# A bounded forget gate as a clamped logit with two softplus terms, and feed-forward products over high and low rows at once as 512 columns

## The reference

```python
log_f = jnp.logaddexp(jnp.log(lb), jnp.log1p(-lb) + jax.nn.log_sigmoid(f_logit))
k = -jnp.expm1(log_f)                       # hgrn2_mixer, then cumsum(log_f) and the chunks
...
def swiglu(h, w13, w2):                     # h 256 x 1024, w13 1024 x 5632, w2 2816 x 1024
    gate, up = jnp.split(h @ w13, 2, axis=-1)
    return (jax.nn.silu(gate) * up) @ w2
```

## Time and profile before

| | |
|---|---|
| median of 3 runs | 2272.09 us |
| the profiled execution's own time | 2272.5 us |
| its span | 2270.7 us |
| PE busy | 2141.9 us, 94% |
| DVE busy | 1372.8 us, 60% |
| ACT busy | 996.0 us, 44% |
| mean granted clock of PE | 0.981 of 2.4 GHz |

### The profile page before, as it was taken

One profiled execution on the slowest core, in us unless ns is written; L12 is line 12 of the kernel. 1 busy time (PEld: TensorE's weight loads), 2 busy tenths in 40 slices (PEclk: granted clock), 3 DMA queues, 4 the chain that ended last, 5 costly groups with the idle time before them and its releaser, 6 DMA issues.

```text
span 2270.7 us, 29738 instructions
## 1 busy us (share of the span) xinstructions
PE 2141.9 (94%) x12707; PEld 1879.8 (83%) x12707; DVE 1372.8 (60%) x1667; ACT 996.0 (44%) x1324; POOL 99.7 (4%) x121
## 2 busy tenths in 40 slices
PE   6999999899798999899999999999998998999998
PEld 5988878888787998687778799989986877877997
DVE  4657865757876555555675555565555666745554
ACT  4544535344444434444444444443434443544432
POOL 0100100100010000000000000000000000000000
PEclk9999999999999999999999999999999999999999
DMA  7453234353235555435545355555544444543552
GB/s 247 131 188 118 87 130 168 111 189 116 70 130 184 180 188 174 136 113 164 193 147 180 114 201 186 196 176 187 185 154 139 135 163 168 185 149 134 191 186 93
DMA packets 192412, 356.84 MB, mean 157 GB/s; under 512 B 8284, under 2 KB 85144, under 8 KB 192280
## 3 DMA queue, kind: packets, MB, share of 16 engines
q1 hardware_dynamic: 189400, 344.46, 45.3%
q0 software_dynamic: 2880, 10.49, 1.4%
HBM read 353.87 MB, written 1.05 MB: 156 GB/s over the span
## 4 chain that ended last, share of the span: by engine, by line
PE 80%; DVE 10%; ACT 4%; issue 3%; DMA 1%; POOL 1%; SPq 0%; POOLq 0%; ACTq 0%; DVEq 0%
PE bank L1864 14%; PE bank L1860 14%; PE bank L1870 14%; PE bank L1887 8%; PE bank L1884 8%; PE bank L1890 8%; DVE raw_r L2334 3%; PE bank L1908 3%; PE bank L2028 2%; PE bank L1925 2%; ACT high L2137 2%; PE bank L1899 1%; PE bank L1946 1%; POOL stat L2824 1%; DVE units L2430 1%
## 5 line engine op out<-in xcount | busy, mean ns | idle before, releaser
L2334 DVE TENSOR_TENSOR raw_r<-raw,high 128x2048 fp32r<-128x2048 f32 (+1 forms) x308 | 694.8, 2273 | 99.6 <-ACT high L2137 99.6
L2137 ACT ACTIVATE high<-raw 128x2048 fp32r<-128x2048 f32 (+1 forms) x308 | 581.2, 1896 | 258.8 <-PE bank L1870 218.5
L1860 PE MATMUL bank<-high,units_r 128*128 128x512 f32 x1648 | 663.9, 403 | 21.3 <-DVE units L2790 11.7
L1864 PE MATMUL bank<-high,units_r 128*128 128x512 f32 x1648 | 651.6, 395 | 24.2 <-DVE units_r L2355 12.4
L1870 PE MATMUL bank<-raw_r,units_r 128*128 128x512 f32 x1648 | 443.9, 391 | 0.2
L1884 PE MATMUL bank<-units_r,high 128*128 128x256 f32 x1600 | 399.1, 285 | 0.0
L1887 PE MATMUL bank<-units_r,high 128*128 128x256 f32 x1600 | 395.8, 283 | 0.0
L1864 PEld LDWEIGHTS bank<-high,units_r 128*128 128x128 f32 x1648 | 314.2, 191 | 92.6 <-DVE units_r L2358 16.0
L1860 PEld LDWEIGHTS bank<-high,units_r 128*128 128x128 f32 x1648 | 313.5, 190 | 88.9 <-issue 21.3
L1870 PEld LDWEIGHTS bank<-raw_r,units_r 128*128 128x128 f32 x1648 | 312.2, 190 | 67.3 <-DVE raw_r L2334 1.6
L1884 PEld LDWEIGHTS bank<-units_r,high 128*128 128x128 f32 x1600 | 308.0, 193 | 1.3
(11 more groups left out here) (247 smaller groups left out, 1849.1 us busy)
## 6 DMA issues: line engine op xcount, KB each, us to landing
raw<-in_ffn_w_dram SPq DMA_DIRECT2D x132, 1024.0 KB, 5.1
raw<-in_w_in_dram SPq DMA_DIRECT2D x108, 1024.0 KB, 5.1
raw<-in_w_out_dram SPq DMA_DIRECT2D x24, 1024.0 KB, 5.0
raw<-in_cross_wkv_dram SPq DMA_DIRECT2D x16, 1024.0 KB, 5.0
raw<-in_w_branch_dram SPq DMA_DIRECT2D x12, 1024.0 KB, 4.9
raw<-in_cross_wq_dram SPq DMA_DIRECT2D x8, 1024.0 KB, 5.2
...
```

The lines of the kernel that those rows point to most:

```text
L1860: pe.matmul(o, h.high(k0 + k)[:, span], p.hi[k][:, cols], start=start and k == 0, stop=False, skip_group_check=True)
L1864: pe.matmul(o, h.low(k0 + k)[:, span], p.hi[k][:, cols], start=False, stop=False, skip_group_check=True)
L2137: done = act.activation(high, raw, ACT.Copy)
L2334: done = dve.tensor_tensor(low, raw, high.bitcast(F32), ALU.subtract)
```

## The change

In the feed-forward parts, `up(j)` uses a new step `wide` instead of `ch`. The high weights stream 512 columns in one matmul, the high rows and the low rows together (`whole` makes one operand from the two units; `pairs` now sorts them by number so that the distance is positive), and the two results stand side by side in a bank. The 8 matmuls with low weights stay at 256 columns. So a tile has 16 matmuls instead of 24 and fills a bank alone. A new step `fold` adds the halves: ACT copies the right half out, DVE adds the left half to it. Tanh, SiLU and `glu` then read a unit instead of a bank. `up` takes four banks at a time instead of two.

In the gate of layer 1, log f is written as clamp(f, ln lb, 0) - ln(1+exp(-|f|)) + ln(1+exp(-|f - ln lb|)): ACT makes, beside ln(1+exp(-|f|)), also ln(1+exp(-|f - ln lb|)) for each bank, with a third table of bounds `NEG_LNLB`; DVE clamps the logit with two `tensor_scalar` of 256 for each bank, and `bounded` is three DVE operations on 128 x 1024 in one step. `gate_f` has two rests instead of five. One more unit (`t2`) is taken.

```diff
+    def whole(self, k, units_r):
+        a, b = (u.i for u in self.pairs[k // 4])
+        return units_r[:, a:b + 1:b - a, k % 4 * 256:k % 4 * 256 + 256]
...
-        return Rows([(self.U.take(), self.U.take()) for _ in range(n)])
+        return Rows([sorted((self.U.take(), self.U.take()), key=lambda u: u.i) for _ in range(n)])
...
+    def mm_wide(self, name, p, h, banks):
+        for c in range(p.n // P):
+            self.work += p.k * (512 + 256)
+            self.do("wide", name=name, p=p, c=c, bank=banks[c], h=h, ends=c == p.n // P - 1)
+            if c == p.n // P - 1:
+                self.done(p)
+            yield 0
+
+    def fold(self, name, need, banks, dst, after):
+        for c, b in enumerate(banks):
+            self.do("fold", name=name, c=c, need=(need, c), bank=b, dst=dst[:, c * 256:c * 256 + 256], after=after)
+            self.B.give(b, ("folded", name, c))
+        return ("folded", name, len(banks) - 1)
...
             def gate_f():
+                t2 = bounds = None
+                if l == 1:
+                    t2 = U.take()
+                    bounds = [a[:, 4 * hg:4 * hg + 4] for a in (LNLB, LN1M, NEG_LNLB)]
                 for q, (b, pr) in enumerate(fb):
-                    do("forget", name=H, q=q, need=pr, bank=b, k_=k_, tl=tl, tc=tc, lns=q == 0, last_set=q == 1 and l == 0)
+                    do("forget", name=H, q=q, need=pr, bank=b, k_=k_, tl=tl, tc=tc, t2=t2, bounds=bounds)
                     B.give(b, ("logf", H, q))
                     yield "rest"
                 if l == 1:
...
-                    do("bounded", name=H, phase=0, k_=k_, tl=tl, tc=tc, bounds=bounds)
-                    yield "rest"
-                    do("bounded", name=H, phase=1, k_=k_, tl=tl, tc=tc, bounds=bounds)
-                    yield "rest"
-                    do("bounded", name=H, phase=2, k_=k_, tl=tl, tc=tc, bounds=bounds)
+                    do("bounded", name=H, k_=k_, tl=tl, tc=tc, t2=t2, bounds=bounds)
+                    U.give(t2, ("bounded", H))
...
-            bg, bu = B.take(), B.take()
-            yield from plan.mm_ch(f"{N}.g{j}", plan.weight(w13, 0, 8, 256 * j, 256), h, [bg])
-            s = plan.silu(f"{N}.s{j}", [("prod", f"{N}.g{j}", 0)], tmp.ap[:, 0:512], bg.ap, tmp.after)
-            B.give(bg, s)
...
+            bg = [B.take(), B.take()]
+            ((_, p),) = plan.weight(w13, 0, 8, 256 * j, 256)
+            yield from plan.mm_wide(f"{N}.g{j}", p, h, bg)
+            g_ = plan.fold(f"{N}.g{j}", ("prod", f"{N}.g{j}"), bg, tmp.ap[:, 0:512], tmp.after)
+            s = plan.silu(f"{N}.s{j}", [g_], tmp.ap[:, 512:1024], tmp.ap[:, 0:512], tmp.after)
+            bu = [B.take(), B.take()]
...
+    def wide(name, p, c, bank, h, ends, **_):                      # PE
...
+            pe.matmul(bank.ap.rearrange("p (a s) -> p a s", a=2), p.hi[k][:, c * P:c * P + P], h.whole(k, m.units_r),
+                      start=k == 0, stop=False, skip_group_check=True)
+        hold.wait_ge(*at(("wlow", p.i)))
+        for k in range(p.k):
+            product = pe.matmul(bank.ap[:, 0:256], p.lo[k][:, c * P:c * P + P], h.high(k), start=False,
+                                stop=k == p.k - 1, skip_group_check=True)
...
+    def fold(name, c, need, bank, dst, after, **_):                # ACT
...
+        act.activation(dst, bank.ap[:, 256:512], ACT.Copy).then_inc(*mark(s.acopy, ("half_out", name, c)))
...
+            for i in range(2):                                     # ACT, forget
+                c = q * 2 + i
+                beyond = act.activation(t2.ap[:, c * 256:c * 256 + 256], bank.ap[:, i * 256:i * 256 + 256], ACT.Abs,
+                                        bias=bounds[2][:, c:c + 1], scale=1.0)
...
+            act.activation(t2.ap[:, sl], t2.ap[:, sl], ACT.Exp, bias=0.0, scale=-1.0).then_inc(*mark(s.expd))
+            hold.wait_ge(*last(s.expd))
+            act.activation(t2.ap[:, sl], t2.ap[:, sl], ACT.Ln, bias=1.0, scale=1.0).then_inc(
...
+                clamped = dve.tensor_scalar(tc.ap[:, c * 256:c * 256 + 256], bank.ap[:, i * 256:i * 256 + 256],
+                                            bounds[0][:, c:c + 1], 0.0, ALU.max, ALU.min)
...
+    def bounded(name, k_, tl, tc, t2, bounds, **_):                # DVE
+        hold.wait_ge(*at(("logf", name, 1)))
+        dve.tensor_tensor(tc.ap, tc.ap, tl.ap, ALU.subtract).then_inc(*mark(s.vstep))
+        dve.tensor_tensor(h3(k_.ap, 4), h3(k_.ap, 4), bc(bounds[1], 256), ALU.subtract).then_inc(
...
+        dve.tensor_tensor(tc.ap, tc.ap, t2.ap, ALU.add).then_inc(*mark(s.vout, ("bounded", name)))
...
+    def fold(name, c, bank, dst, **_):                             # DVE
+        hold.wait_ge(*at(("half_out", name, c)))
+        dve.tensor_tensor(dst, bank.ap[:, 0:256], dst, ALU.add).then_inc(*mark(s.vout, ("folded", name, c)))
```

102 lines of the change are left out of this document (51 added, 51 removed).

## The result

The changed kernel takes 2255.52 us (median of four runs, 2254.12 to 2256.11) against 2273.06 for the kernel before on the same basis (four runs, 2271.39 to 2276.54). The ratio is 0.992, 95% interval 0.9903 to 0.9937, so it is faster by 0.6 to 1.0%. The forecast was 2251.4, range 2244 to 2264. The profiled execution has a span of 2253.9 us, 16.8 less than before; 21.1 was forecast.

A forecast was written before the change was run, and what follows sets the result against it. PE, busy 94% of the span, was taken as the bound. From 2272.5 us, -15.4 (feed-forward), -2.7 and -0.5 (first heads) and -2.5 (second heads) sum to -21.1, giving 2251.4 us, range 2244 to 2264.

The forecast's parts named there:

- The bound and the main mechanism: Feed-forward parts: only PE's pace counts, and fewer matmuls shorten the time; PE busy 140.00 of 140.00 us.
- the 13.3 ns beside its columns: Feed-forward matmuls on PE: each costs a fixed 13.3 ns whatever its width, beside one column per cycle.
- The first rival: Feed-forward: the fixed 13.3 ns doesn't go, so the gate alone gives 2266.8 us; 7% together with the skill-figure case, 2263.9.
- The term of -15.4 us: Feed-forward parts: 144 `wide` tiles at 2.773 us instead of 2.880, 0.107 us less each, 15.4 us in all.
- one piece later: Feed-forward: a gate product's bank is wanted again 5.55 us after its last product, so no wait was taken.
- the sign named in the prediction: Feed-forward parts: the forecast counts as wrong if they give less than 13 us, or the time exceeds 2264.
- The term of the first heads, -2.7 and -0.5: Layer 1's gate, first four heads: PE starts at 410.2 instead of 412.87, -2.7 us; the clock after the wait, -0.5.
- The second heads, -2.5: Layer 1's gate, second four heads: earlier waits grow, later ones go, net -2.5 us, bounds +5 and -6.
- The second rival: Layer 1's gate goes the wrong way: scan ahead of scores costs 5 us, first heads give nothing; 2262.1 us, 12%.
- the sum of both terms, -5.7: Layer 1's gate: -2.7 and -0.5 for the first four heads with -2.5 for the second four.
- ACT and DVE at nothing, no bank dry: Feed-forward: the new copies and additions hide behind PE, cost nothing; banks running dry, 2312 us, was given 5%.

The follow-up runs named there:

- halves: The changed kernel with each matmul of 512 columns made as two of 256 with the same weight; 2267.16 us, ratio to the kernel before 0.9971.
- gate_only: The changed kernel with the feed-forward code of before put back, so only the gate is changed; 2266.62 us, ratio to the kernel before 0.9975.
- rests: The changed kernel with three resting places put ahead of the bounded gate of layer 1; 2255.72 us, ratio to the kernel before 0.9922.
- contig: The changed kernel with the 512 columns read contiguously from one unit, so wrong rows are multiplied; one run of 2254.72 us.
- wide_only: The changed kernel with the old gate put back, so only the feed-forward parts are changed; 2261.71 us, ratio to the kernel before 0.9951.
- no_fold: The changed kernel without the fold's copies on ACT and additions on DVE, PE's work the same; one run of 2257.23 us.
- the three loaded kernels: The changed kernel with the fold's copy moved or repeated, as dve_fold, dve_stress and act_stress; one run each, 2257.65, 2282.27 and 2260.90 us.
- act_stress: The changed kernel with the fold's copy on ACT made four times; one run of 2260.90 us.
- grouped: The changed kernel with both tiles' matmuls of 512 columns run before both tiles' of 256 for each weight piece; 2255.78 us, ratio to the kernel before 0.9921.
- dve_fold: The changed kernel with the fold's copy made by DVE instead of ACT; one run of 2257.65 us.
- dve_stress: The changed kernel with the fold's copy made by DVE instead of ACT, three times over; one run of 2282.27 us.

## Why the prediction was right, and what it had wrong

**The bound and the main mechanism: right.** PE's pace alone counts in the feed-forward parts, a removed matmul takes the 13.3 ns beside its columns with it, less the cost of a change of width, and the gain is 0 when the matmuls are put back with all else left as it is (`halves`). The first rival is out. By the fixed remainder that the Trainium skill gives for warm matmuls back to back ("TensorE: Matmul & The Clock Gate", section "Wait — 56ns, not 53.3ns?", about 2.5 ns) the 1152 removed matmuls would be worth an estimated 2.9 us. `halves` against the changed kernel measures 12.8, so the runs don't agree with it for this pattern, in which each matmul loads its weights.

**The term of -15.4 us: too large.** A `wide` tile was costed at 8 x 226.7 + 8 x 120.0 = 2.773 us and takes 2.79. The 226.7 came from a `tok` block that follows another one, a row in which the width doesn't change; a `wide` tile changes it every 16 matmuls. The first `tok` block behind a `ch` tile would have shown it: 2.74 us. All 36 `up` together went from 414.9 to 402.0 us, 12.8 less (the medians of one, 11.515 and 11.148 us, would make it 13.2). Of the other 0.5 us to the 12.3 found, 0.35 are a wait behind the first fold (740.74), and the rest I can't assign. The wait stands where the prediction's "one piece later" doesn't hold: the second `up` of a part takes the banks of the product right before it. So the sign named in the prediction, less than 13 us from these parts, came true, by 0.7 us, from a mis-sized term.

**The term of the first heads, -2.7 and -0.5: a little small in sum, and the two parts are off by more.** PE starts `same` 4.0 us earlier, not 2.7. ACT's table load starts at 400.44 instead of 401.0 to 401.2, and the second high part didn't wait for its piece (3.70 us for both from 404.14), so that the copies begin at 407.74. Behind this wait of 1.76 us the clock stayed up: over 412 to 424 it is 1.00, before 0.79. That gave 1.9 us more by 411.10 (417.04 before), where -0.5 was taken. But a new wait of 1.76 us at 419.85, which was not foreseen, took them back, and from there on the lead is 4.0 us. That the clock could be left at -0.5 without harm is luck.

**The second heads, -2.5: right** (-2.55 measured), with waits grown to 5.25 and 4.06 and those behind them gone, as told. The second rival, the gate going the wrong way, is out with `gate_only` at 0.9975. `rests` supports the reason, eight passes of 1024 become five. But the same gate is worth -3.7 in all in `halves`, -5.7 in `gate_only`, -6.6 in the changed kernel and -7.6 in `contig`, and the old gate of `wide_only` is 1.5 us ahead of its like: the sum of both terms, -5.7, is met no better than that.

**ACT and DVE at nothing, no bank dry: right** but for the 0.35 us above, by `no_fold` and the three loaded kernels. The end of a part cost nothing either: PE's wait there is 1.73 us before and after. `act_stress` shows that it isn't far from costing something.

**Missing: the +2.3 us between the feed-forward parts of layer 0.** The stretch from the wait of 1.73 us behind the first part to the one of 2.89 us ahead of the second (898.48 to 1297.51 before, 889.24 to 1290.59 after) holds the same instructions. It takes 399.0 us before, 399.0 in `gate_only` and 398.8 in `halves`, in which the feed-forward parts are as long as before, and 401.4 after, 401.4 in `wide_only` and `contig`, 401.6 in `grouped`. The same stretch of layer 1 takes 398.1 to 398.5 in all of these but `grouped` (398.9). The granted clock is at half for 20.5 us of the stretch in both traces, but at other places: before for 6.8 us at 932.4 and 1133.7 and for 3.4 at 976.7 and 1154.2, after for 3.4 at 925.6 and 1253.3 and for 6.8 at 966.6 and 1127.0. What counts is what PE has to do there. At 1253.3 it has matmuls back to back. The first row is the changed kernel, the second the same place before (first the length and PE's busy time with its matmuls, at the end the granted clock, DMA share and GB/s):

```profile
1253.30:1256.70 3.40, 3.33 (x15) 3.36 (x16) 0.00 (x0) 0.46 (x1) 0.00 (x0) 0.50 0.45 171
1261.60:1265.00 3.40, 3.34 (x28) 3.20 (x29) 0.41 (x1) 1.04 (x2) 0.00 (x0) 1.00 0.45 172
```

At 1154.2 before, it is where the changed kernel waits 0.91 us for a low part (1148.60) that the kernel before reached later without a wait. Both traces have the same 1880 matmuls in this stretch. Set side by side, the steps from start to start that lie in a half-clock stretch of one of the two or of both add up to +2.4 us, and all others to -0.05. It isn't the new form that costs it: `dve_fold` and `dve_stress` have the same `wide` tiles, their clock falls at 1149.5 and 1155.6 as in the kernel before, and the stretch takes 399.9 and 399.4 us; `no_fold` and `rests`, with a fall at 1254.5 and 1255.3, take 401.7 and 401.6. What sets the places I didn't test.

Together: -6.56 - 12.3 + 2.3 - 0.2 = -16.8. The sum missed by 4.3 us of span: 3.1 in the feed-forward term, 2.1 in the stretches between, and -0.9 in the gate. The gate's 0.9 and the 2.1 are of the size by which executions differ. Of the 3.1, 2.6 are the price of a `wide` tile, which the rows of before could have given.
